# The feed-forward's output product as seven chained products of a 2x2x2 partition, and keys and scores one step earlier in the retention

## The reference, cut to what matters

```
def swiglu(h, w_in, w_out):
    g, u = jnp.split(h @ w_in, 2, axis=-1)
    return (jax.nn.silu(g) * u) @ w_out
...
x = layer_norm(ALPHA * x + g2 * swiglu(x * (1.0 + sc2) + sh2, w_ffn_in[l], w_ffn_out[l]), ln2_w[l], ln2_b[l])
```

```
scores = jnp.einsum('bcnhd,bcmhd->bchnm', qc, kc) * intra.astype(dt)
o_intra = jnp.einsum('bchnm,bcmhe->bcnhe', scores, vc)
kv = jnp.einsum('bcmhd,bcmhe,hm->cbhde', kc, vc, zeta.astype(dt)).astype(jnp.float32)
...
o_cross = jnp.einsum('bcnhd,cbhde,hn->bcnhe', qc, prev.astype(dt), xi.astype(dt))
```

## Time and profile before

| what | value |
|---|---|
| median of 3 runs | 2132.29 us (2129.41 to 2133.77) |
| the profiled execution's own time | 2132.22 us |
| its span in the trace | 2130.4 us |
| granted TensorE clock, mean over the span | 0.976 of full speed |
| TensorE busy | 2014.5 us, 95% |
| VectorE busy | 1349.7 us, 63% |
| ScalarE busy | 757.2 us, 36% |
| GpSimd busy | 449.7 us, 21% |

### The profile page before, as it was taken

The page is one execution under the profiler, slowest core; times in us unless marked ns, Lnnn a source line. Parts: engine busy times, 40 slices in busy tenths (PEclk is TensorE's granted clock), DMA queues, the critical chain, the costliest instruction groups (busy, mean ns, idle before and its releaser), DMA issues. The chain is left out here.

```text
span 2130.4 us, 27279 instructions
## 1 busy us (share of the span) xinstructions
PE 2014.5 (95%) x10285; PEld 1508.8 (71%) x10285; DVE 1349.7 (63%) x2390; ACT 757.2 (36%) x1523; POOL 449.7 (21%) x512
## 2 busy tenths in 40 slices
PE   6999999998988999999999998889999788989998
PEld 3854474566877888888888787757888665668775
DVE  6673595548997555554532277489999688661523
ACT  2222111246144333333421234364121446760425
POOL 1910000143300000000000012125667351200210
PEclk9999999999999999999999999999999999999999
DMA  8443110113331322222611442112111002021101
GB/s 327 171 124 123 48 54 26 31 50 129 97 121 60 114 71 83 89 84 89 223 60 44 152 167 96 52 51 79 50 49 40 29 3 78 1 105 75 40 0 79
DMA packets 127542, 179.24 MB, mean 84 GB/s; under 512 B 14686, under 2 KB 81566, under 8 KB 124090
## 3 DMA queue, kind: packets, MB, share of 16 engines
q1 hardware_dynamic: 121242, 156.60, 22.7%
q0 software_dynamic: 6080, 20.98, 2.5%
q10 hardware_dynamic: 96, 0.02, 0.0%
HBM read 153.12 MB, written 23.13 MB: 83 GB/s over the span
## 5 line engine op out<-in xcount | busy, mean ns | idle before, releaser
L2996 DVE TENSOR_SCALAR_CACHE_REDUCE pj_junk<-NM,prm 128x384 uint8<-128x384 f32 (+1 forms) x186 | 163.7, 943 | 1.1
L1759 PE MATMUL ps<-pj_part,h 128*128 128x512 f32 x384 | 153.1, 399 | 0.2 <-ACT PJ L2853 0.2
L1760 PE MATMUL ps<-pj_part,h 128*128 128x512 f32 x384 | 150.3, 391 | 0.0
L1761 PE MATMUL ps<-pj_part,h 128*128 128x512 f32 x384 | 150.2, 391 | 0.0
L2938 POOL TENSOR_TENSOR pj_part<-pj_raw,pj_part 128x512 fp32r<-128x512 f32 x64 | 84.7, 1326 | 157.4 <-ACT pj_part L2848 156.1
L1759 PE MATMUL ps<-w_end,se_hT 128*128 128x512 f32 x256 | 106.9, 418 | 0.4 <-DVE se_hT L3720 0.4
L1041 PE MATMUL ps<-mx_w,HT 128*128 128x272 f32 (+1 forms) x320 | 106.5, 493 | 0.0
L1761 PE MATMUL ps<-w_end,se_hT 128*128 128x512 f32 x256 | 99.9, 390 | 0.0
L1760 PE MATMUL ps<-w_end,se_hT 128*128 128x512 f32 x256 | 99.7, 389 | 0.0
L2848 ACT ACTIVATE pj_part<-pj_raw 128x512 fp32r<-128x512 f32 x64 | 40.6, 639 | 149.3 <-DMA pj_raw<-in_w_in 146.3
L1759 PEld LDWEIGHTS ps<-pj_part,h 128*128 128x128 f32 x384 | 72.4, 189 | 29.1 <-issue 14.2
(11 more groups left out here) (865 smaller groups left out, 5376.0 us busy)
## 6 DMA issues: line engine op xcount, KB each, us to landing
s_wm<-in_w_mod SPq DMA_DIRECT2D x16, 1024.0 KB, 4.7
pj_raw<-in_w_in SPq DMA_DIRECT2D x64, 256.0 KB, 2.6
ff_hr<-ff_hid SPq DMA_DIRECT2D x40, 256.0 KB, 4.6
mod_w<-in_w_mod SPq DMA_DIRECT2D x8, 1024.0 KB, 8.7
ff_w0p<-in_w_ffn_in SPq DMA_DIRECT2D x22, 256.0 KB, 3.2
ff_w1p<-in_w_ffn_in SPq DMA_DIRECT2D x22, 256.0 KB, 3.3
ff_hid<-ff_d POOLq DMA_DIRECT2D x20, 256.0 KB, 2.3
ff_hid<-ff_c POOLq DMA_DIRECT2D x19, 256.0 KB, 4.4
```

The lines of the kernel that those rows point to most:

```text
L1759: nc.tensor.matmul(out, w[0], x[0], start=first, stop=False)
L1760: nc.tensor.matmul(out, w[0], x[1], start=False, stop=False)
L1761: return nc.tensor.matmul(out, w[1], x[0], start=False, stop=last)
L2996: last = v.tensor_scalar(junk[:, packed(j + 2)], x, bound(j), 0.0, ALU.is_ge, ALU.add, accum_out=cnt[:, j:j + 1])
```

## The change

The second product is partitioned 2x2x2 as well: the contraction in halves of 11 blocks (`NJ`), the output columns in two halves, the token rows in two halves. Instead of eight quarter products there are seven, in the order 1, 2, 6, 5, 3, 7, 4 (`OUT_ORDER`), each 11 units of 12 matmuls: 77 units. Products 1, 2 and 3 use plain weight quarters. Products 4 to 7 use sums of weight quarters, which GpSimd makes during the first product (`make`) out of four tiles that SyncE loads (`made_load`) and stores to a DRAM tensor `ff_sums` afterwards (`made_store`). The hidden rows of products 1, 2 and 4 are plain quarters; those of 5, 6, 3 and 7 are the four sums S1 to S4, which VectorE makes during the earlier products (`first_sum` to `fourth_sum`). Rows are no longer split once and kept: each of the 77 units splits its own row tile (`step_high`, `step_low`), next to its weight tile. PSUM banks are carried from product to product, and partial results are added into `ynT` on VectorE (`evict_added`). Evictions wait for single banks. The normalisation of the first four token tiles lies beside products 7 and 4. `MIX_AHEAD` is 3 in place of 4. In the retention, TensorE makes the scores of tile i + 1 and turns tile i + 2 ahead of its wait for tile i's masked scores, and GpSimd weights the keys of tile i + 1 behind the gate of tile i.

```diff
-OUT_UNITS = [(g, f) for g in range(3) for f in range(NF)]
+NJ = NF // 2
+OUT_ORDER = (1, 2, 6, 5, 3, 7, 4)
+OUT_UNITS = [(p, j) for p in OUT_ORDER for j in range(NJ)]
-MIX_AHEAD = 4
+MIX_AHEAD = 3
...
+            def made_load(j):
+                if j >= 2:
+                    sp.wait_ge(made_st[j % 2], made_base[j % 2] + 64 * (j // 2))
+                for n, (f, c) in enumerate(((j, 0), (j, HALF), (NJ + j, 0), (NJ + j, HALF))):
+                    sp.dma_start(made[j % 2][n][:], w2[f][:, c:c + HALF]).then_inc(made_in[j % 2], 16)
+
+            def made_store(j):
+                sp.wait_ge(psum, 4 * j + 4)
+                b11, b12, b21, b22 = made[j % 2]
+                for p, t in ((4, b21), (5, b11), (6, b22), (7, b12)):
+                    sp.dma_start(sums[p - 4, j], t[:]).then_inc(made_st[j % 2], 16)
...
                 pair_load(f)
+                if 0 <= f - 10 < NJ:
+                    made_store(f - 10)
+                if 0 <= f - 8 < NJ:
+                    made_load(f - 8)
...
+                j = q - NSLOT
+                if j < NJ:
+                    back_load(21, j)
+                    if j < NJ - 2:
+                        back_load(22, j)
...
+            def make(j):
+                b11, b12, b21, b22 = made[j % 2]
+                pool.wait_ge(made_in[j % 2], 16 + 64 * (j // 2 + 1))
+                g.tensor_tensor(b11[:], b12[:], b11[:], ALU.subtract).then_inc(psum, 1)
+                g.tensor_tensor(b12[:], b22[:], b12[:], ALU.subtract).then_inc(psum, 1)
+                pool.wait_ge(psum, 4 * j + 2)
+                g.tensor_tensor(b22[:], b22[:], b11[:], ALU.subtract).then_inc(psum, 1)
+                pool.wait_ge(psum, 4 * j + 3)
+                g.tensor_tensor(b21[:], b21[:], b22[:], ALU.subtract).then_inc(psum, 1)
...
+                if 0 <= f - 7 < NJ:
+                    make(f - 7)
...
+            def step_high(q):
+                p, j = OUT_UNITS[q]
+                if q == 8:
+                    act.wait_ge(mm, NI)
+                elif q >= 12:
+                    act.wait_ge(om, q - 3)
+                rows_wait(act, p, j)
+                nc.scalar.activation(step_tile(q)[0][:], rows_in(p, j)[:], ACT.Copy).then_inc(ahi, 1)
...
+                if 0 <= u - NI - 9 < NJ:
+                    first_sum(u - NI - 9)
+                if 0 <= u - NI - 18 < NJ:
+                    second_sum(u - NI - 18)
+                if 0 <= u - NI - 19 < NJ:
+                    fourth_sum(u - NI - 19)
+                if 0 <= u - NI - 33 < NJ:
+                    third_sum(u - NI - 33)
...
+                pe.wait_ge(alo, q + 1)
+                r, wh, wl = out_slots[q % NSLOT]
+                xh, xl = step_tile(q)
+                for n in range(4):
+                    bank = n if p in (1, 6, 7, 4) else 4 + n
+                    if j == 0:
+                        bank_free(p, n)
+                    for i, (w, x) in enumerate(((wh, xh), (wh, xl), (wl, xh))):
+                        last = nc.tensor.matmul(K.bank[bank][:], w[:, n * P:(n + 1) * P], x[:], start=(j == 0 and i == 0 and p in (1, 2, 5)),
+                                                stop=(j == NJ - 1 and i == 2), skip_group_check=True)
...
-        for i in range(NT):
-            s = i % 2
+
+        def scores(i):
...
             prepare(2 * i + 1)
+            if i + 1 < NT:
+                scores(i + 1)
+            if i + 2 < NT:
+                turn(i + 2)
             pe.wait_ge(S["prob"], i + 1)
```

More of the change, by code:

```diff
@@ new lines, in stage_join_ffn, with rows_in @@
+    A22 = quarter("q", [62] + [116 + 2 * j for j in range(NJ - 3)]) + [place(1, f) for f in (NS, NS + 1)]
+    A22b = A21[0:NJ - 2] + A22[NJ - 2:]
+    S1 = A22[0:NJ - 2] + quarter("s", (108, 110))
+    S2 = quarter("t", (104, 106, 18, 74))
+    S3, S4 = A11, A12
+    def rows_in(p, j):
+        return {1: A11, 2: A12, 6: S2, 5: S1, 3: S4, 7: S3, 4: A22b}[p][j % 4 if p == 6 else j]
+    step_kb = [164 + 4 * n for n in range(8)] + [148 + 4 * n for n in range(4)]
+    step_tiles = [[K.at(f"ff_x{n}{m}", kb + 2 * m, [P, HALF], FR) for m in range(2)] for n, kb in enumerate(step_kb)]
@@ L1833, in use_of @@
[L1833 to L1834 removed]
+    made = [[K.at(f"ff_m{s}{n}", kb, [P, HALF]) for n, kb in enumerate(of)] for s, of in enumerate(((64, 66, 68, 70), (112, 114, 4, 6)))]
     K.ynT = K.at("ynT", 164, [P, 2, KT, HALF])
@@ L1877, in stage_join_ffn, with arrived @@
     sum4_at[at_unit[1, 4] - 1] = 4
-    SIDE = NI + 2 * NF
+    SIDE = NI + 5 * NJ
+    arrivals = [(11, j) for j in range(NJ)] + [(12, j) for j in range(NJ - 2)] + [(x, j) for j in range(NJ) for x in (21, 22) if x == 21 or j < NJ - 2]
+    arrivals += [(4, j) for j in range(NJ - 2)]
+    arrival = {x: m for m, x in enumerate(arrivals)}
+    def arrived(engine, x, j):
+        m = arrival[x, j]
+        engine.wait_ge(back_in[m % NB], 16 * (m // NB + 1))
     def stored_wait(engine, half, f):
@@ L2022, in _, with rows_wait, bank_wait @@
                 pool.dma_start(K.fe_x[i % 2][:], K.x1[(i + 2) * P:(i + 3) * P, :]).then_inc(K.fe_y_in[i % 2], 16)
+        def rows_wait(engine, p, j):
+            if p == 1:
+                arrived(engine, 11, j)
+            elif p == 2 and j < NJ - 2:
+                arrived(engine, 12, j)
+            elif p == 2:
+                engine.wait_ge(hd0, NJ + j + 1)
+            elif p == 6:
+                engine.wait_ge(s2_done, s2_base + j + 1)
+            elif p == 5:
+                engine.wait_ge(s1_done, s1_base + j + 1)
+            elif p == 3:
+                engine.wait_ge(psum, s4_base + j + 1)
+            elif p == 7:
+                engine.wait_ge(psum, s3_base + j + 1)
+            elif j < NJ - 2:
+                arrived(engine, 4, j)
+            else:
+                engine.wait_ge(hd1, NJ + j + 1)
+        def bank_wait(engine, p, n):
+            o = OUT_ORDER.index(p)
+            if n < 3:
+                engine.wait_ge(oh, 3 * o + n + 1)
+            else:
+                engine.wait_ge(om, NJ * (o + 1))
         def in_tiles(u):
@@ L3126, in tensor @@
                     d = slice(RD * a, RD * (a + 1))
-                    mm = nc.tensor.matmul(K.bank[3 + a][:, j * P:(j + 1) * P], kT[s][d, j, :], qT[s][d, j, :], start=True, stop=True)
+                    mm = nc.tensor.matmul(K.bank[3 + a][:, j * P:(j + 1) * P], kT[i % 2][d, j, :], qT[i % 2][d, j, :], start=True, stop=True)
             mm.then_inc(S["smm"], 1)
-            if i + 1 < NT:
-                turn(i + 1)
+        scores(0)
+        turn(1)
+        for i in range(NT):
+            s = i % 2
             if i == 0:
```

318 lines of the change are left out of this document (166 added, 152 removed), and 4 rows, old and new, of the table hid_kb.

## The result

The changed kernel takes 2100.93 us, the median of 4 runs (2100.26 to 2101.47); the kernel before, run beside it, takes 2132.47 us (4 runs, 2129.41 to 2133.77). The ratio is 0.9854 with a 95% interval of 0.9837 to 0.9871: 31.5 us faster, where 35.0 were forecast. The profiled execution took 2101.14 us and has a span of 2099.2 us, 31.2 less than before, at the same mean clock of 0.976.

A forecast was written before the change was run, and what follows sets the result against it. TensorE, busy 95% of the span, was taken to bound the kernel. The terms -29.9 + 0 + 0 + 0.5 + 0.3 + 1.5 - 0.7 + 0.3 - 7 gave -35.0 us, from 2132.22 to 2097 us; range 2089 to 2112.

The forecast's parts named there:

- Matmuls, -29.9: Second product: 924 matmuls instead of 1056, 132 fewer at 0.2266 us each, 29.9 us off TensorE.
- GpSimd's sums, 0: First product: 44 sums may hold VectorE up to 5.2 us a block, covered by its lead of two units; cost 0.
- rival D: First product: GpSimd's sums hold VectorE, which holds TensorE, 1 to 2 us a block, 11 to 22 us; chance 0.10.
- Transfers and the start of the second product, 0 and +0.5: First product's added loads and stores cost 0; row and weight loads at the second product's start cost +0.5 us.
- Products 1 to 3, +0.3, and 7 and 4, +1.5: Second product: VectorE's splits, sums and evictions cost +0.3 us; later doubled splits, norms and GpSimd's low parts +1.5 us.
- Rival C: Second product: late row tiles, or VectorE falling behind in products 7 and 4, cost 8 to 18 us; chance 0.13.
- The end, -0.7 and +0.3: Second product's end: one eviction instead of two behind the last matmul, -0.7 us; `MIX_AHEAD` 3 moves GpSimd work onward, +0.3 us.
- The retention, -7: Masked scores of tile 1 to tile 7: keys leave the path, turns of 9.3 us, 56 us instead of 63.2.
- Rival B: Retention gains nothing, as the wait for keys becomes one for the masked scores; 2104 us; chance 0.12.

The follow-up runs named there:

- e3: The changed kernel without GpSimd's 44 sums of weight tiles, which are stored as loaded: 2099.24 us, ratio 0.984 to the kernel before.
- e8: The changed kernel with four more GpSimd operations per block on a weight tile, each waiting for the one before: 2099.81 us, ratio 0.9842 to the kernel before.
- e6: The changed kernel with GpSimd's keys ahead but TensorE's order of before in the retention: 2101.67 us, ratio 0.9856 to the kernel before.
- e7: The changed kernel with TensorE's scores ahead but GpSimd's order of before in the retention: 2103.86 us, ratio 0.9869 to the kernel before.
- e1: The changed kernel with the whole retention of the kernel before: 2102.4 us, ratio 0.9859 to the kernel before.
- e12: The changed kernel with ScalarE's decay of the state first in each retention turn: 2104.23 us, ratio 0.9864 to the kernel before.
- e5: The changed kernel with ScalarE's eviction of `at_v` ahead of the next tile's queries and keys: 2102.46 us, ratio 0.9861 to the kernel before.

## Why the prediction was right

*Matmuls, -29.9.* Measured -30.8 from the first matmul of the second product to the last (before from 1044.5 to 1289.01 us, after 213.7). The 0.9 us more are two waits of the kernel before for `ff_o4l` (1.2 us) against one of 0.3 for `ff_x` now.

*GpSimd's sums, 0.* Right, and by the reason given. VectorE is held for 4.2 us a block, of 5.2 at most; `ff_w05` was to be ready at about 868.1 us and was at 868.7; the next split was done at 870.4, for matmuls due near 873.0. What I had not seen is `ff_w10l`, which is held longest (3.44 us), and that VectorE's later wait for ScalarE (3.79 us without the sums) takes the delay up again. e3 rules out rival D: without the sums the time is less by 1.7 us, within the scatter, and D asked for 11 or more. e8 agrees.

*Transfers and the start of the second product, 0 and +0.5.* Measured 0: in the windows TensorE is without a pause from 1044 to 1200 us, at up to 214 GB/s.

*Products 1 to 3, +0.3, and 7 and 4, +1.5.* Over-costed. One wait of 0.3 us, near the end of product 4, is left of both. I had GpSimd's three low parts hold VectorE 3.3 us; they held it 1.9 (1.69 and 1.62 against 0.69 each), and the lead of two units covered it. Rival C did not come.

*The end, -0.7 and +0.3.* The step that failed. "Behind the last matmul VectorE evicted two; now one: -0.7 us" takes the last eviction for what the boundary waits for. By the traces it is GpSimd's store and reload of token tile 3, 6.0 to 6.4 us ahead of the next stage in every one, and the change moved it closer to the last matmul: +1.5 where -0.4 was forecast. The rows for it stood in the trace of before; I had read VectorE's end of the stage and not GpSimd's queue.

*The retention, -7.* Right in kind, too large. It gave 4.4 us from tile 1 to tile 7. The keys were the path (e6, e7). "What is late next is VectorE" fits the trace as well, though no run tests it. The 9.3 us a turn was the mis-sized term. It came from 8.3 us of work plus something for two turns with a long mask third. Measured are three turns of 8.4 to 8.8 and three of 10.8 to 11.3, 9.8 on average. I had left out that VectorE also waits in its own chain: 4.0 us for the decay and 1.6 for the square roots (ScalarE's `prm`). Rival B was wrong as a whole, but the half of the change that it speaks of, the scores ahead, did gain nothing.

*Sum.* -35.0 forecast, -31.2 in the span. Of the 3.8 us between them, the boundary has 1.9, the retention 2.5, what lies behind it 1.8 (1.6 of it the slow matmuls of the attention) and the stretch ahead of the retention 0.6; the second product gave 3.1 us back, 0.9 by waits that went and the rest by small costs that never came. The total is nearer than its parts: errors of both signs met in it, and so its closeness is in part luck.

## What to carry to other kernels

When the engine that bounds a stage has no idle time in it, counting its instructions gives the gain within a microsecond; the errors sit in what happens at the stage's edges and in the loops where nobody is busy all the time. Ask at a boundary which queue ends last, the slow one with the stores and reloads included, and not only which engine does the last arithmetic. And in a loop where two chains are close, taking away the next wait in line (the decay) can cost more than it frees, because the engine that serves it serves the other chain as well: read both chains' slack first.

## What the runs showed of the hardware

GpSimd held VectorE's operations with two SBUF inputs for 45.8 us in the first product and nothing came of it: the splits were done ahead of their matmuls, and VectorE would have waited for ScalarE soon after. Two of GpSimd's operations back to back cost `ff_w10l` 2.8 us; with a wait between them, in e8, the same operation lost 1.5. Yet the pair without a wait later in e8's block let VectorE in between, so the wait isn't all that decides.

The granted clock was lower where TensorE waited for the keys. Windows of the retention in the kernel before (busy time of PE, granted clock, DMA share, GB/s):

```profile
1694.00:1704.00 10.00, 7.04 (x43) 0.85 0.00 0
...
1724.00:1734.00 10.00, 8.06 (x60) 0.89 0.01 2
```

and the least busy one of the changed kernel up to the last tile:

```profile
1654.00:1664.00 10.00, 8.04 (x60) 1.00 0.01 2
```

In the changed kernel the granted clock is 1.00 in all six windows from 1654 to 1714 us. e1 and e7, which have the waits for the keys, fall to 0.90 in a window too. But idle time alone doesn't bring it on. In e12 TensorE waits 11.5 us for `at_v`, and yet its least busy window, like the five behind it, has the full clock:

```profile
1655.00:1665.00 10.00, 7.15 (x54) 1.00 0.01 2
```

In e5 it fell to 0.66 at 1654 to 1664 us and to 0.54 at 1714 to 1724, though TensorE was busy 9.29 of 10 us in the second of these windows. What brought that on, these runs don't show.
